# Hybrid GLA/Hyena layer on one core: the first three blocks in a new order, and a quarter of the second shift's sums moved to units 137 to 158

## What is computed

```python
sh1, sc1, g1, sh2, sc2, g2 = modulation(c, w_ada, b_ada)        # silu(c) @ w_ada + b_ada
csh1, csc1, ...            = modulation(c_ctx, w_ada, b_ada)
hc = rmsnorm(ctx, norm_pre_mix) * (1 + csc1) + csh1
s_f, s_b = context_states(hc, w_in, ...)                        # k, v, decay of the context
hx = rmsnorm(x, norm_pre_mix) * (1 + sc1) + sh1
x = x + g1 * rmsnorm(mixer(hx, s_f, s_b, ...), norm_post_mix)    # GLA and Hyena, merged
hx = rmsnorm(x, norm_pre_ffn) * (1 + sc2) + sh2
x = x + g2 * rmsnorm(swiglu(hx, ffn_gate, ffn_up, ffn_down), norm_post_ffn)
```

## Time and profile before

| | us |
|---|---|
| median of 3 runs | 1625.83 (1625.36 to 1626.21) |
| the profiled execution | 1625.28 |
| its span in the trace | 1623.5 |
| PE busy | 1587.5 (98%) |
| DVE, ACT, POOL busy | 1101.5, 749.4, 81.0 |
| moved by DMA | 377.74 MB, mean 233 GB/s |

### The profile page before, as it was taken

One profiled execution on the slowest core, in us unless ns is written; L12 is line 12 of the kernel. 1 busy time (PEld: TensorE's weight loads), 2 busy tenths in 40 slices (PEclk: granted clock), 3 DMA queues, 4 the chain that ended last, 5 costly groups with the idle time before them and its releaser, 6 DMA issues.

```text
span 1623.5 us, 22521 instructions
## 1 busy us (share of the span) xinstructions
PE 1587.5 (98%) x8524; PEld 1302.6 (80%) x8524; DVE 1101.5 (68%) x1320; ACT 749.4 (46%) x901; POOL 81.0 (5%) x156
## 2 busy tenths in 40 slices
PE   6999999999999999999998999999999999999998
PEld 3556677888888888888887888888888888888886
DVE  3677777678789868778777666666666555555556
ACT  5442326643444434444446544555545544444444
POOL 0011120000000000100000000000000000000000
PEclk9999999999999999999999999999999999999999
DMA  9989958666577768966885777777776665565653
GB/s 332 327 299 379 326 191 280 187 202 202 178 244 222 229 200 267 297 225 217 292 298 178 233 237 231 244 230 235 237 234 198 186 191 197 193 193 192 194 193 121
DMA packets 264769, 377.74 MB, mean 233 GB/s; under 512 B 14161, under 2 KB 223420, under 8 KB 263164
## 3 DMA queue, kind: packets, MB, share of 16 engines
q1 hardware_dynamic: 243008, 297.57, 58.2%
q0 software_dynamic: 20800, 78.91, 14.3%
q10 hardware_dynamic: 892, 0.33, 0.1%
HBM read 372.57 MB, written 4.19 MB: 232 GB/s over the span
## 4 chain that ended last, share of the span: by engine, by line
PE 92%; DVE 3%; DMA 2%; ACT 1%; issue 1%; ACTq 0%; DVEq 0%
PE ps L1664 39%; PE ps L1671 19%; PE ps L1679 9%; PE ps L1681 8%; PE ps L1680 8%; PE ps L1604 2%; DMA a2k<-in_w_ada 1%; DVE acck L1048 1%; PE ps L1803 1%; PE ps L1815 0%; PE ps L1594 0%; PE ps L1841 0%; DVE lo L1116 0%; PE ps L1766 0%; PE ps L1833 0%
## 5 line engine op out<-in xcount | busy, mean ns | idle before, releaser
L1441 DVE TENSOR_TENSOR lo<-raw,hi 128x1024 fp32r<-128x1024 f32 x252 | 308.3, 1224 | 247.9 <-ACT hi L879 247.5
L1664 PE MATMUL ps<-hx,hi 128*128 128x512 f32 x1392 | 438.0, 396 | 1.5 <-DVE lo L1441 0.8
L879 ACT ACTIVATE hi<-raw 128x1024 fp32r<-128x1024 f32 x252 | 266.7, 1060 | 317.0 <-PE ps L1671 203.9
L625 ACT ACTIVATE hi<-raw 128x1024 fp32r<-128x1024 f32 x224 | 236.6, 1060 | 277.9 <-PE ps L1671 163.9
L1664 PE MATMUL ps<-hxc,hi 128*128 128x512 f32 x1088 | 346.0, 399 | 0.0
L1116 DVE TENSOR_TENSOR lo<-raw,hi 128x1024 fp32r<-128x1024 f32 x224 | 269.5, 1220 | 67.3 <-ACT hi L625 67.2
L1671 PEld LDWEIGHTS ps<-hx,lo 128*128 128x128 f32 x1408 | 264.5, 188 | 62.5
L1671 PE MATMUL ps<-hx,lo 128*128 128x256 f32 x1408 | 276.6, 278 | 0.0
L1671 PEld LDWEIGHTS ps<-hxc,lo 128*128 128x128 f32 x1088 | 204.4, 188 | 48.3
L1664 PEld LDWEIGHTS ps<-hx,hi 128*128 128x128 f32 x1392 | 212.0, 189 | 2.8 <-DVE lo L1441 1.0
L1671 PE MATMUL ps<-hxc,lo 128*128 128x256 f32 x1088 | 213.9, 278 | 0.0
(11 more groups left out here) (323 smaller groups left out, 1685.8 us busy)
## 6 DMA issues: line engine op xcount, KB each, us to landing
raw<-in_w_in SPq DMA_DIRECT2D x160, 512.0 KB, 4.6
a2raw<-in_w_ada POOLq DMA_DIRECT2D x96, 512.0 KB, 5.1
raw<-in_ffn_gate SPq DMA_DIRECT2D x88, 512.0 KB, 4.4
raw<-in_ffn_up SPq DMA_DIRECT2D x88, 512.0 KB, 4.4
raw<-in_ffn_down SPq DMA_DIRECT2D x88, 512.0 KB, 4.6
ada_raw<-in_w_ada SPq DMA_DIRECT2D x64, 512.0 KB, 10.1
a2k<-in_w_ada POOLq DMA_DIRECT2D x32, 512.0 KB, 6.7
raw<-in_w_out SPq DMA_DIRECT2D x32, 512.0 KB, 5.3
```

The source lines that it names most:

```text
L625: nc.scalar.activation(high_of(uu), raw[:, slot_of(uu), :], ACT.Copy).then_inc(hi_done, 1)
L879: nc.scalar.activation(hi[:, slot, :], raw[:, uu % RING, :], ACT.Copy).then_inc(hi_done, 1)
L1441: V.tensor_tensor(lo[:, uu % RING, :], raw[:, uu % RING, :], hi[:, uu % 4, :].bitcast(f32), SUB).then_inc(lo_done, 1)
L1664: mm(bank(b + t), (hi[:, uu % 4, :] if w_h is None else w_h)[:, c0:c0 + P], feat[:, k, :], start=first, stop=False)
```

## The change

In the blocks, PE's, ACT's, DVE's, SP's and POOL's streams are reordered; no matmul of the products is added or removed.
- A fourth `ada_raw` buffer, used once, in the room of raw slots 3 and 4: units 0 to 3 are loaded without a wait, and SP's queue goes on to weights and tokens.
- PE's start: the fillers and `ada_unit(0)` come before `turn 1` and `sine 0`; `sine 2` moves behind idx 1 of block 0. As many fillers in all (24).
- The four `filter_pair`s move from idx 0, 2, 4, 6 of block 1 to idx 4 and 6 of block 1 and idx 1 and 3 of block 2; the spectra to idx 5 to 11 of block 2 and idx 0 of block 3. DVE's `columns` stands right behind its `kv_evac`, ahead of `unit_low` and `a2`.
- Of the 32 accumulations of `sh2`, 24 stay in the blocks (`A2_KV`), and 8 (a = 56 to 63) go into a sum of their own, `acck2`, at units 137 to 144, with 12 of `sc2` behind them up to unit 157; eight more small matmul pairs in `column_sums` reduce `acck2`. `g1` is now a = 24 to 55, at the same units as before. The rest of `sc2` stands at 162, 172, 182 and from 192 on.
- The transfer of the Fourier matrix on POOL waits for piece 20 (before: 12), and `a2_load` starts after piece 26.
- DVE's wait for `j_cols` behind `column_sums` moves behind two small sums.

```diff
         ada_raw = [at(f"ada_raw{i}", O_M + o * KB, [P, 4, 512]) for i, o in enumerate((0, 8, 48))]
+        ada_raw.append(at("ada_raw3", O_RAW + 12 * KB, [P, 4, 512]))
...
+        acck2 = at("acck2", O_M + 52 * KB, [P, 1024])
...
-        A2_KV = [(), (7, 9, 11), (1, 3, 5, 7, 9, 11), (1, 3, 5, 7, 9, 11), (1, 9, 11),
-                 (1, 3, 5, 7, 9, 11), (1, 3, 5, 7, 9, 11), (1, 3)]
+        NKS = 24
+        A2_KV = [(), (), (7, 9, 11), (1, 4, 6, 9, 11), (1, 4, 9, 11), (0, 1, 2, 4, 9, 11),
+                 (2, 6, 10), (1, 2, 4)]
         A2_AT = ([28 + int(2.4 * a) for a in range(19)] + [81, 86, 91, 96, 99, 102, 105, 108, 110, 112, 119, 121, 123]
-                 + [138 + int(1.7 * a) for a in range(13)] + [160 + 6 * a for a in range(5)]
-                 + [198 + int(1.6 * a) for a in range(14)])
+                 + [137 + int(1.1 * a) for a in range(20)] + [162, 172, 182]
+                 + [192 + int(1.6 * a) for a in range(17)])
...
-        AFTER = [{3: "a", 5: "xa", 7: "at", 8: "a", 9: "c"},
-                 {2: "a", 4: "a", 6: "a", 8: "a", 9: "tc"},
-                 {0: "a", 1: "at", 3: "a", 5: "a", 7: "c", 10: "a"}]
+        AFTER = [{5: "axa", 7: "at", 8: "a", 9: "c"},
+                 {1: "a", 3: "a", 5: "a", 7: "a", 8: "t", 9: "c"},
+                 {0: "a", 1: "a", 3: "a", 5: "a", 6: "t", 7: "c", 10: "a"}]
...
-        FILT_AFTER = [{}, {0: 0, 2: 1, 4: 2, 6: 3}] + [{}] * (NB - 2)
-        SPEC_AFTER = {0: 0, 1: 1, 2: 2, 3: 3, 4: 4, 6: 5, 8: 6, 11: 7}
+        FILT_AFTER = [{}, {4: 0, 6: 1}, {1: 2, 3: 3}] + [{}] * (NB - 3)
+        SPEC_AFTER = {(2, 5): 0, (2, 6): 1, (2, 7): 2, (2, 8): 3, (2, 9): 4, (2, 10): 5, (2, 11): 6,
+                      (3, 0): 7}
...
-            for n in range(3):
+            for n in range(4):
                 ada_load(n)
-            ada_load(3)
             weight_load(0)
             weight_load(1)
             sp.dma_start(toks[:, 2, :], ctxt[0:P, :]).then_inc(s_ctx[0], 16)
             weight_load(2)
             sp.dma_start(toks[:, 3, :], ctxt[P:2 * P, :]).then_inc(s_ctx[1], 16)
-            for b in range(NB - 1):
+            for n in range(4, 8):
+                ada_load(n)
+            weight_load(3)
+            ada_load(8)
+            ada_load(9)
+            weight_load(4)
+            filter_load()
+            ada_load(10)
+            weight_load(5)
+            ada_load(11)
+            weight_load(6)
+            weight_load(7)
...
-            pool.wait_ge(kv_pe, 12)
+            pool.wait_ge(kv_pe, 20)
             pool.dma_start(cp[:, K_FWD:K_SEL], k_pack[:, K_FWD:K_SEL]).then_inc(s_fwd, 16)
...
             start_step("sine", 0)
-            start_step("sine", 1)
             rows(0)
             cut_high(0)
             first_modulate(0, 0)
             first_modulate(1, 0)
+            start_step("sine", 1)
...
             for b in range(1, NB):
                 for idx in range(12):
                     kv_evac(b, idx)
-                    if b == 1 and idx == 0:
-                        unit_low(5)
+                    if b < NB - 1 and idx == MOD_AT[b]:
+                        columns(b + 1)
+                    if b == 1 and idx in (1, 5):
+                        unit_low(4 + idx // 5)
...
-            dve.wait_ge(j_cols, 1)
-            link(V.tensor_tensor(modc[:, 4, :], bank(0)[:, 0:KD], col1[:, B_SC2:B_SC2 + KD], ADD))
...
             add_part(37, 36, st[:, 37:38]).then_inc(j_sum, 1)
+            dve.wait_ge(j_cols, 1)
+            V.tensor_tensor(modc[:, 5, 8:16], modc[:, 5, 8:16], bank(0)[:, KD:KD + 8], ADD)
...
+                for j in range(8):
+                    ins = mm(bank(0)[:, KD + j:KD + j + 1], acck2[:, P * j:P * (j + 1)],
+                             ones[:, 0:1], start=True, stop=True)
...
             start_step("turn", 0)
+            keep_running(6)
+            pe.wait_ge(t_sem["a"], 1)
+            ada_unit(0)
             start_step("turn", 1)
             start_step("sine", 0)
-            pe.wait_ge(t_sem["a"], 1)
-            ada_unit(0)
-            keep_running(4)
+            keep_running(3)
             ada_unit(1)
-            keep_running(4)
+            keep_running(5)
             start_step("sine", 1)
+            ada_unit(2)
             turn_tokens(0, range(2))
             turn_tokens(1, range(2))
-            ada_unit(2)
-            keep_running(6)
             ada_unit(3)
             keep_running(2)
-            start_step("sine", 2)
             columns(0)
```

More of the change, by code:

```diff
@@ L199, in layer @@
         s_win = sem("s_win")
-        ada_in = [sem(f"ada_in{i}") for i in range(3)]
+        ada_in = [sem(f"ada_in{i}") for i in range(4)]
         ada_mm, ada_rows = sem("ada_mm"), sem("ada_rows")
@@ L426, in weight_load, with filter_load @@
                 sp.dma_start(dst, srcw).then_inc(arrival(uu)[0], 16)
-            for n in range(3):
+            def filter_load():
+                for half in range(2):
+                    sp.dma_start(outw[HID * half:HID * (half + 1), :],
+                                 out_w[:, HY * half:HY * (half + 1)]).then_inc(s_win, 16)
+                sp.dma_start(win[:], k_win.rearrange("(t p) n -> p t n", p=P)).then_inc(s_win, 16)
+            for n in range(4):
                 ada_load(n)
-            ada_load(3)
             weight_load(0)
@@ L517, in _ @@
             pool.wait_ge(kv_ev, 12 * (NB - 1))
-            for a in range(32, 53):
+            for a in range(NKS, 45):
                 a2_load(a)
@@ L532, in _ @@
             pool.dma_start(grow[:], b_ada[:, 2 * D:3 * D].broadcast_to([P, D])).then_inc(s_row[0], 16)
-            for a in range(61, 64):
+            for a in range(53, 56):
                 a2_load(a)
@@ L536, in _ @@
             pool.dma_start(acc[:], n_post_mix.broadcast_to([P, D])).then_inc(s_row[1], 16)
-            for a in range(64, 84):
+            for a in range(56, 84):
                 a2_load(a)
@@ L697, in _ @@
             kv_copy(7)
+            cut_high(3)
             kv_copy(8)
@@ L708, in _ @@
                 cut_high(3 * b + 3)
-                if b == 2:
-                    for m in range(5):
-                        spectrum(m)
+                if b == 3:
+                    spectrum(7)
                 cut_high(3 * b + 4)
@@ L1877, in _ @@
                         rank_products(3).then_inc(mm_done, NKV)
-                    for what in AFTER[b].get(idx, ""):
+                    for j, what in enumerate(AFTER[b].get(idx, "")):
                         if what == "a":
-                            ada_unit(nth_unit(b, idx))
+                            ada_unit(nth_unit(b, idx) + AFTER[b][idx][:j].count("a"))
                         elif what == "s":
                             pe.wait_ge(ada_mod, NB)
-                            shift_sums(32).then_inc(ada_cols, 1)
+                            shift_sums(NKS).then_inc(ada_cols, 1)
                         elif what == "x":
@@ L1893, in _ @@
                         filter_pair(FILT_AFTER[b][idx])
-                    if b == 2 and idx in SPEC_AFTER:
-                        spectrum(SPEC_AFTER[idx])
+                    if (b, idx) == (0, 1):
+                        start_step("sine", 2)
+                    if (b, idx) in SPEC_AFTER:
+                        spectrum(SPEC_AFTER[b, idx])
             for uu in range(NKV, NM - NW):
```

165 lines of the change are left out of this document (83 added, 82 removed).

## The result

The changed kernel takes 1639.15 us (median, 1633.74 to 1640.65), the kernel before 1626.02 beside it: a ratio of 1.0073, 95% interval [1.0058, 1.0087]. The change makes the kernel 0.7% slower. The forecast was 1622.1, in a range up to 1628.0: wrong, and on the other side.

The account below looks back on a forecast made before the run. PE is busy 1587.5 of 1623.5 us, so time comes only from its waits and clock. 3.8 + 6.5 + 0.3 - 5.3 - 1.6 = 3.7 us less than 1625.83 gives 1622.1, range 1613.5 to 1628.0.

Parts of the forecast that it names:

- start: Kernel start: fourth buffer and earlier PE work bring the first piece at 27.6 us, 3.8 us less.
- blocks 0 to 2: PE's waits around the filters and the slow clock behind them go, 6.5 us less, bounds 4 and 7.5.
- waits at the start of block 7: PE's 1.5 + 0.7 us of wait at the start of block 7 go, 2.2 us less.
- sums of blocks 5 and 7: Sums of `sh2`: PE waits 2.2 us instead of 0.3 in block 7, 1.9 us more; block 5 not named.
- units 137 to 158: Denser accumulations outrun the two-buffer transfer chain at a 5.3 us landing; PE waits for `lo`, 5.3 us more.
- unit 201: `x1` is issued 3.1 us later, a = 84's strip lands behind it, PE waits: 1.6 us more, bounds 0 and 4.
- column sums: Eight more matmul pairs, 1.8 us, lie in the 3.6 us that PE waits for `xn` anyway: no cost.
- Blocks 3 to 7: Waits at block 7's start go, 2.2 us, against 1.9 us more at its sums: 0.3 us less.
- Rival 3: The clock falls at the sums of block 7, price 3.4 us, time 1625.5; chance 0.18.
- rival 4: The blocks' new order only moves the waits and the clock falls as before: 1627.0 us; chance 0.08.
- Rival 1: The dense stretches at units 137 to 157 and around `x1` are hidden, 5.3 + 1.6 us come back: 1615.2; chance 0.26.
- rival 2: Two-buffer chain at units 137 to 157 with a 6.2 us landing costs 13.4 us, not 5.3: 1630.2; chance 0.12.

Follow-up runs that it names:

- both: Changed kernel with b57's accumulations in blocks 2 to 7 and a wider pitch of those from unit 137 on: 1614.23 us, 0.9929 of the kernel before.
- after_again: The changed kernel measured once more, nothing altered: 1638.68 us, 1.0074 of the kernel before.
- b57: Changed kernel with 3, 6, 6, 3 and 6 accumulations in blocks 2 to 6, none in block 7: 1623.84 us, 0.9992 of the kernel before.
- gap201: b57 with no accumulations at units 196 to 200 during the residual's transfer, the dense ones at 137 to 157 kept: 1620.46 us, 0.9972 of the kernel before.
- pack_late: Changed kernel with the constants' transfer and the gate weights behind it issued only after the 24th accumulation: 1635.72 us, 1.0065 of the kernel before.
- keep7: Changed kernel with 32 unused unit-matrix matmuls before PE's wait at block 7's sums: 1634.00 us, 1.0055 of the kernel before.
- b5: Changed kernel with six accumulations each in blocks 3 and 4, three in block 5, block 7 unchanged: 1634.38 us, 1.0052 of the kernel before.

## Why the prediction was wrong, by its own steps

| step | predicted us | measured us | from |
|---|---|---|---|
| start | -3.8 | -4.0 | first piece 27.38 against 31.37 |
| blocks 0 to 2 | -6.5 | -6.7 | block 4 at 134.17 against 144.84, less the start |
| waits at the start of block 7 | -2.2 | -2.0 | `both` at unit 24: 12.7 in all |
| sums of blocks 5 and 7 | +1.9 | +14.8 | `after_again` less `b57` |
| units 137 to 158 | +5.3 | +6.2 | `gap201` less `both` |
| unit 201 | +1.6 | +3.4 | `b57` less `gap201` |
| column sums | 0 | 0 | 7.25 against 7.23 us |
| sum | -3.7 | +11.7 | medians: +12.9 |

The terms come from medians and from single traces, so the last line closes only to 1.2 us. Block 3 itself starts 11.5 us earlier (109.05 against 120.56 us), but 0.8 of that is gone by the start of block 4, since the last spectrum now stands in block 3; so the second row is taken there. The row for unit 201 is the one of least worth: in the seven profiles with a wait there PE loses 2.7 to 7.0 us at units 191 to 223.

**The step that failed is "Blocks 3 to 7".** It put the sums of `sh2` at +1.9 us in block 7 and said nothing of those in block 5; the runs showed +14.8 us at the two. Three things were wrong in it.

First, a place was left out. The change moves the first sums to block 5's idx 7 and puts accumulations 12 to 14 at idx 0, 1 and 2, with 15 at idx 4. By the rule that the prediction itself wrote for units 137 to 158 (0.3 + landing + 1.28 us for every second accumulation) two steps lie between the end of 11 (160.8 us) and that of 15. With 3.9 us for a landing that is 2 x 5.5 = 11.0 us, 171.8: free of a wait by 3.5 us. With the 7.0 us measured it is 17.2 us, 178.0, and PE waits from 175.3. The rule was there and was not applied. Applied with the 3.9 us, or with the 5.3 of the earlier trace rows (174.6), it would still have shown no wait. What it needed was the landing in the blocks, and the trace of the kernel before had it: from 0 to 240 us, all 32 strips,

```profile
a2k<-in_w_ada POOLq DMA_DIRECT2D x32, 512.0 KB, 6.7
```

and 7.1 us for the nine issued at 100 to 140 us. With 6.7 the chain ends at 177.4, a wait of 2.1 us. The 3.9 of the earlier trace rows is one strip at the end of block 7, one of the fastest of the 32.

Second, a term was mis-sized. In block 7 the chain was right to 0.5 us up to the issue of the last strip (219.03; with T = 212.74, accumulation 21 done at T + 6.5 and 0.3 to the issue, 219.5) and PE was ready at 222.3 (predicted 222.5). But the landing took 6.8 us and not 3.9, so the wait was 5.0 and not 2.2. In the kernel before, the constants were issued 1.4 us behind the strip of the earlier trace rows (225.74 against 224.38), now they are 0.5 us behind it, with the eight gate weights at once after them. The bounds of "1 and 3" were bounds on PE's and DVE's times; the landing had none, although and the earlier trace rows show 5.3 and 6.2 us for the same 512 KB elsewhere. Up to 2.0 us of it come from the constants (`pack_late`); the rest stays open.

Third, the clock. Rival 3 happened, at both sums, and it had a chance of 0.18. In `after_again` the granted clock at 225 to 245 us is 0.74, and the fall costs 20 x 0.26 = 5.2 us instead of 3.4; in `pack_late` it costs 1.8. The waits at sums were followed by a fall in every profile that has one: in seven of seven at block 5 (2.4 to 3.0 us of wait) and in six of six at block 7 (3.1 to 5.0), but not with `keep7`'s matmuls in the wait; with a wait of 0.2 us or none there was none.

**Right:** the start to 0.2 us and by its mechanism; blocks 0 to 2 to 0.2 us, with no wait for `filt_o` and no fall at 62 to 71 us, so rival 4 is out (the wait for `hxc` at block 2 is 0.3 us, not 1.0); the column sums; `x1` issued 3.1 us later (793.77 us with PE 5.2 us late at unit 190, so 788.6). **Right in kind, small in size:** units 137 to 158. In the first profile PE loses 4.8 us there with a landing of 5.3 us, where 5.3 were summed. That sum has a slip: from a = 62 to a = 64 it goes 6.3 us (644.7 to 651.0) where its own rule gives 6.9, so by the rule it is 5.9. What it lacked is the clock, again: behind a wait of 2.2 to 2.4 us at unit 143 it falls in `b57`, `gap201` and `keep7` (not behind 2.4 and 2.6 in `b5` and `after_again`), and in `b57` PE loses 8.3 us in the stretch. The same at 201: the waits are 1.8 to 4.0 us (predicted 1.6), and a fall comes on top in five of seven profiles. Rival 1 is out (these stretches aren't hidden), and rival 2 too for the changed kernel (the landing is 5.0 to 5.3 us in its two profiles, not 6.2).

What the change was worth is the upper part of the table: 12.7 us of start and blocks, 12.5 predicted. All of that and 12 us more were lost at four places where an accumulation comes sooner than its strip can land. `both`, which has none of the four, is 11.2 us faster than the kernel before.

## What to carry to other kernels

Where one of two buffers is refilled only after its last use, lay every place that has a deadline against the chain of issue, landing and use, with the landing that the trace shows where the engines are as busy as they are there, and not with that of the row nearest in time. Price a wait of TensorE of some 2 us or more as the wait plus a fall of its clock (1.7 to 5.2 us here), and take it away rather than fill it: the waits taken out were worth 13.8 us at unit 24, the one filled with unused matmuls 1.1 to 1.3, since they ran 2.7 us past the end of the wait. When an edit frees time, ask what the next fixed appointment is (here sums that need 16 and 24 strips) and whether its supply became faster as well.

## What the runs showed of the hardware

**The landing of the same 512 KB strip** on POOL's queue takes 3.9 us at 224 us, 4.8 to 6.8 for the last strip in block 7 of the changed kernel and four of its variants, 4.8 to 6.0 (medians at 637 to 687 us, `keep7` and `b57`) at units 137 to 158, 6.7 in the blocks of the kernel before and 7.0 in block 5 of the changed one (medians, with `ada_raw` and weights in flight; DMA share 1.02 at 100 to 160 us before), and 8.4 beside the residual's 2 MB (a median again; the strip issued right behind it, at 795.59 us, takes 13.5). The Trainium skill gives a fixed cost and a bandwidth for one transfer ("DMA: Bandwidth & Descriptors", section "Anatomy of one DMA — SWDGE (gpsimd) path"), an estimate of 3.2 us for this size. No full strip of any run here reached it: the fastest took 3.7 us. The sum went wrong not on the 3.2 but on taking one fast strip, 3.9 us, for one in a loaded stretch.

**Whether the clock falls behind a wait of some 2 us is not fixed.** Take each profile's longest wait for `lo` at 560 to 700 us, and the one at 201. Of eight such waits of 1.8 to 2.8 us four were followed by a fall (1.8, 2.2, 2.4 and 2.4 us) and four not (2.4, 2.4, 2.6 and 2.8); all four of 3.4 to 4.0 us were. So two executions of one kernel, 1633.7 and 1638.2 us, differ mostly by what happens at 201: a wait of 2.4 us without a fall, and one of 4.0 with it. The Trainium skill says that what watches the activity runs free of the kernel ("TensorE: Matmul & The Clock Gate", section "What's actually happening"); that falls come in one execution and not in another after like waits agrees with it.
